# Ranking experts in halves of 64 tokens, with the first tile's rows turned before the next tile's query

## The reference, cut to what matters

```
q = (hc @ w_query).reshape(128, 8, 2, 64)                 # 8 heads, two half keys
s = einsum('chpd,hpnd->chpn', q, sub_keys)                # 128 scores for each half key
s_top, i_top = top_k(s, 16)
cand = s_top[:, :, 0, :, None] + s_top[:, :, 1, None, :]  # 16 x 16 pairs per head
cand_id = i_top[:, :, 0, :, None] * 128 + i_top[:, :, 1, None, :]
best, pos = top_k(cand, 16)
eid = take_along_axis(cand_id, pos); gate = softmax(best)
u = take(u_tab, eid)                                      # 8 x 16 rows of 1024 for each token
act = gelu(einsum('chkd,cd->chk', u, hc)) * gate
out = einsum('chk,chkd->cd', act, take(v_tab, eid))
```

## Time and profile before

| | |
|---|---|
| median of 3 runs | 3320.21 us |
| profiled execution: span, first to last instruction | 3317.3 us |
| the same against the median | 2.9 us below |
| PE busy | 2336.2 us (70%) |
| DVE busy | 1679.4 us (51%) |
| POOL busy | 1480.8 us (45%) |
| moved by DMA | 1047.22 MB, 316 GB/s on average |

### The profile page before, as it was taken

The page is one execution under the profiler, slowest core; times in us unless marked ns, Lnnn a source line. Parts: engine busy times, 40 slices in busy tenths (PEclk is TensorE's granted clock), DMA queues, the critical chain, the costliest instruction groups (busy, mean ns, idle before and its releaser), DMA issues.

```text
span 3317.3 us, 36982 instructions
## 1 busy us (share of the span) xinstructions
PE 2336.2 (70%) x12540; PEld 1281.0 (39%) x12540; DVE 1679.4 (51%) x4368; ACT 558.5 (17%) x1179; POOL 1480.8 (45%) x1577
## 2 busy tenths in 40 slices
PE   7899867898999888995465444447898545444444
PEld 5477624365777545764121000004587400000000
DVE  2521576644233586436965444443712795444444
ACT  2320231401100235102240000002511210000000
POOL 1100044444444444430666777771000167777775
PEclk9999978799999898997575555557899755555555
DMA  8967679899999896991999999993233299999998
GB/s 307 352 209 267 238 269 350 304 354 378 362 365 366 323 347 235 363 334 64 375 349 388 409 409 409 409 409 111 70 114 134 84 379 409 409 409 406 409 409 341
DMA packets 325915, 1047.22 MB, mean 316 GB/s; under 512 B 27424, under 2 KB 38752, under 8 KB 325728
## 3 DMA queue, kind: packets, MB, share of 16 engines
q0 software_dynamic: 240192, 880.90, 69.2%
q1 hardware_dynamic: 85536, 163.95, 14.1%
HBM read 1043.70 MB, written 1.05 MB: 315 GB/s over the span
## 4 chain that ended last, share of the span: by engine, by line
PE 49%; DVE 18%; issue 13%; DMA 10%; ACT 3%; PEld 3%; POOL 2%; PEldq 0%; DVEq 0%; ACTq 0%; POOLq 0%
PE ps L404 24%; PE ps L440 12%; DVE UV L1044 8%; DMA UV<-in_v_tab,idxT 7%; PE ps L426 4%; PEld ps L404 3%; ACT arena L1679 2%; PE ps L396 2%; DMA W<-in_w_mod 2%; POOL UV L2157 1%; PE ps L529 1%; PE ps L571 1%; DVE arena L1415 1%; DVE arena L1424 1%; DVE arena L1418 1%
## 5 line engine op out<-in xcount | busy, mean ns | idle before, releaser
L1044 DVE SCALAR_TENSOR_TENSOR UV<-ps,UV 128x1024 f32<-128x1024 f32 x768 | 909.8, 1222 | 833.4 <-PE ps L426 816.3
L2157 POOL DMA_INDIRECT UV<-in_u_tab,idxT x768 | 723.5, 942 | 1182.4 <-DVEq L1510 498.1
L440 PE MATMUL ps<-UV,acts 128*32 128x512 f32 x3072 | 632.5, 908 | 560.3 <-DVE acts L1053 456.6
L2167 POOL DMA_INDIRECT UV<-in_v_tab,idxT x768 | 724.9, 944 | 281.6 <-issue 198.8
L404 PE MATMUL ps<-H,W 128*128 128x256 f32 (+2 forms) x3296 | 668.7, 363 | 36.4 <-ACT H L1679 26.5
L404 PEld LDWEIGHTS ps<-H,W 128*128 128x128 f32 (+1 forms) x3296 | 574.7, 194 | 147.3 <-issue 76.6
L404 PE MATMUL ps<-arena,W 128*128 128x256 f32 (+1 forms) x1632 | 371.6, 385 | 20.4 <-issue 8.6
L440 PEld LDWEIGHTS ps<-UV,acts 128*32 128x32 f32 x3072 | 78.3, 129 | 716.1 <-DVE acts L1053 572.7
L404 PEld LDWEIGHTS ps<-arena,W 128*128 128x128 f32 (+1 forms) x1632 | 304.4, 190 | 103.3 <-issue 53.2
L426 PE MATMUL ps<-hs,selb 32*128 32x512 bf16 x1536 | 208.5, 530 | 153.1 <-DVE UV L1044 153.0
L1679 ACT ACTIVATE gel<-dots 128x2 f32<-128x2 f32 x384 | 77.4, 202 | 1255.9 <-DVE UV L1044 1247.3
(11 more groups left out here) (198 smaller groups left out, 1698.9 us busy)
## 6 DMA issues: line engine op xcount, KB each, us to landing
W<-in_w_in SPq DMA_DIRECT2D x30, 2048.0 KB, 10.1
UV<-in_w_mod POOLq DMA_DIRECT2D x18, 2048.0 KB, 12.3
W<-in_w_ff SPq DMA_DIRECT2D x16, 2048.0 KB, 14.2
UV<-in_w_ada POOLq DMA_DIRECT2D x9, 2048.0 KB, 11.7
W<-in_w_out SPq DMA_DIRECT2D x8, 2048.0 KB, 11.4
W<-in_w_mod POOLq DMA_DIRECT2D x6, 2048.0 KB, 19.9
W<-in_w_query SPq DMA_DIRECT2D x6, 2048.0 KB, 9.2
UV<-in_u_tab,idxT POOLq DMA_INDIRECT x768, 8.8
```

The source lines that it names most:

```text
L440: last = mm(ps[q:q + GROUP, YB, :], acts[:, tok % SLOTS, GROUP - 1 - r:2 * GROUP - 1 - r], Vs[:, tok % SLOTS, hf * 512:(hf + 1) * 512], st ...
L1044: dve.scalar_tensor_tensor(out=Us[:, j, :], in0=ps[:, b:b + 2, :].rearrange("p a b -> p (a b)"), scalar=1.0, in1=Us[:, j, :], op0=MUL, op1 ...
L2157: pool.indirect_dma_start(Us[:, j, :], None, A["u_tab"], off).then_inc(sem(f"u_arrived{j}"), 16)
L2167: pool.indirect_dma_start(Vs[:, j, :], None, A["v_tab"], off).then_inc(sem(f"v_arrived{j}"), 16)
```

## The change

The ranking of a tile is done in two halves r = 0, 1 of 64 tokens. The scores are laid out so that the 128 partitions hold 64 tokens twice, once for each half of the heads; each half has then 8 lists of scores and 4 of pair sums in each partition instead of 16 and 8. A half has 8 steps (two "top", two "pairs", four "keys"), its own turn of expert numbers and gates, and gatherers wait for half a tile. `route_first` ranks only half 0 of tile n before the stream opens; `route_second` begins with half 1 of tile n, beside the stream, and then both halves of tile n + 1. The transposes of tile n's rows now come ahead of the query of tile n + 1, and VectorE and ScalarE make the parts after "top 1" of half 0. The pieces beside the ranking in c0 are placed anew.

```diff
-STEPS = ["residue", "parts", "top 0", ..., "top 3", "pairs 0", ..., "pairs 3", "keys 0", ..., "keys 3", "experts"]
+STEPS = ["top 0", "top 1", "pairs 0", "pairs 1", "keys 0", "keys 1", "keys 2", "keys 3"]
+HALF = P // 2
-                   "n2": [13], "queried": [14, 15], "pairs 0": [16], "pairs 2": [17]}
-        ADDED_AT = {**MODS_AT, "queried": [], "pairs 0": [], "top 1": [14], "top 3": [15], "pairs 2": [16], "keys 1": [17]}
+                   "n2": [13], "queried": [14, 15], "pairs 0": [16], "pairs 1": [17]}
+        ADDED_AT = {**MODS_AT, "queried": [], "top 0": [14], "top 1": [15], "pairs 0": [], "pairs 1": [16], "keys 3": [17]}
 # TensorE
-                while owed[0] >= PACE and seen[0] < min(segment[1], PAIRS * ready[0]):
+                while owed[0] >= PACE and seen[0] < min(segment[1], PAIRS // 2 * ready[0]):
...
-                        last = mm(o[p][:, hh * P:(hh + 1) * P], qp[64 * p:64 * p + 64, h, in_h(n)],
-                                  keys[64 * p:64 * p + 64, h, :], start=True, stop=True)
+                for i in range(4):
+                    for b in range(2):
+                        h, at = 4 * a + 2 * b + i % 2, n % 2 * P + i // 2 * HALF
+                        for p in range(2):
+                            last = mm(o[p][HALF * b:HALF * b + HALF, i * P:(i + 1) * P], qp[64 * p:64 * p + 64, h, at:at + HALF],
+                                      keys[64 * p:64 * p + 64, h, :], start=True, stop=True)
...
-                    beat((STEPS[i], n), (4.4 if i < 6 else 3.2) if n == 1 else 12.4 if i < 6 else 7.6)
+                    beat((step, n, r), {"top": 4.4, "pairs": 3.2, "keys": 2.0}[what] if n < 2 else {"top": 12.4, "pairs": 7.6, "keys": 4.6}[what])
...
-                pe.transpose(o[:, 0:P], eid, ident[:, :])
-                full(pe.transpose(o[:, P:2 * P], gat.rearrange("p a b -> p (a b)"), ident[:, :]), ("ij", n))
+                for b in range(2):
+                    q = slice(HALF * b, HALF * b + HALF)
+                    mm(o[q, 0:HALF], eid[q, f], ident[q, q], start=True, stop=True)
+                    last = mm(o[q, HALF:P], gat.rearrange("p a b -> p (a b)")[q, f], ident[q, q], start=True, stop=True)
...  # route_first
                     scores(n, u)
+                hidden(n, hold)
                 mods_at(tag, "queried")
                 for u in range(2):
                     query(tag, n + 1, u)
-                hidden(n, hold)
-                routes(n)
+                routes(n, 0)
...  # route_second
+                rows_by_pair(n - 1, [0])
+                routes(n - 1, 1, {"top 0": [lambda: rows_by_pair(n - 1, range(1, 8))]})
                 for a in range(2):
-                    rows_by_pair(n - 1, [a])
                     scores(n, a)
                 if tag == "x0":
                     stream("tile 1 done", max(seen[0], 2 * PAIRS + 2))
-                routes(n, {"top 0": [lambda: rows_by_pair(n - 1, range(2, 8))], **beside})
+                for r in range(2):
+                    routes(n, r, beside.get(r, {}))
...
-            BESIDE = {"top 1": [lambda: hidden(1, bank)], "top 2": [lambda: norm("f", "n1"), lambda: rows_after(1)],
-                      "top 3": [lambda: first_products(0)], "pairs 2": [lambda: first_products(1)]}
+            BESIDE = {0: {"top 1": [lambda: hidden(1, bank)], "pairs 1": [lambda: norm("f", "n1"), lambda: rows_after(1)],
+                          "keys 1": [lambda: first_products(0)]}, 1: {"top 0": [lambda: first_products(1)]}}
 # VectorE: every step works on slice hh of 4 heads instead of all 8, for example
-                    sixteen_best(top, tix, sc, [(i, i) for i in range(4 * e, 4 * e + 4)])
+                    sixteen_best(top, tix, sc, [(i, i) for i in range(8 * r + 4 * e, 8 * r + 4 * e + 4)])
...
-                routes(n, 2)
-                hidden(n)
+                routes(n, 0, {"top 1": [lambda: hidden(n)]})   # hidden: residue, wait part2, third part, wait parts_ready
...
+                routes(n - 1, 1)
                 for a in range(2):
                     beat("sc", n, a)
...
+                for r in range(2):
+                    routes(n, r, beside.get(r, {}))
 # ScalarE, route_first
+                hidden(n)
+                beat("ht", n)
                 mods_at(tag, "queried")
                 for u in range(2):
                     query(n + 1, u)
-                hidden(n)
-                beat("ht", n)
-                routes(n)
-                second_part(n)
+                routes(n, 0, {"top 1": [lambda: second_part(n)]})
 # ScalarE, routes: spreads ranks and takes exponentials of one half at a time; route_second as on TensorE
 # GpSimd
-                if 2 * g % P == 0:
-                    pool.wait_ge(sem("idx_ready"), 2 * g // P + 1)
+                if 2 * g % HALF == 0:
+                    pool.wait_ge(sem("idx_ready"), 2 * g // HALF + 1)
```

More of the change, by code:

```diff
@@ L829, in routes @@
-            def routes(n, beside={}):
-                for i in range(2, len(STEPS) - 1):
-                    beat((STEPS[i], n), (4.4 if i < 6 else 3.2) if n == 1 else 12.4 if i < 6 else 7.6)
-                    if n == 0:
-                        mods_at("c0", STEPS[i])
-                    for piece in beside.get(STEPS[i], ()):
+                for i in range(4):
[4 more added lines that the diff above has]
+                                      keys[64 * p:64 * p + 64, h, :], start=True, stop=True)
+                            if (i, b) == (3, 1):
+                                full(last, ("sc", n, a, p))
@@ L836, in routes @@
+                beat(("sc", n, a), 2.0)
+            def routes(n, r, beside={}):
+                for step in STEPS:
+                    what = step.split()[0]
+                    beat((step, n, r), {"top": 4.4, "pairs": 3.2, "keys": 2.0}[what] if n < 2 else {"top": 12.4, "pairs": 7.6, "keys": 4.6}[what])
+                    if (n, r) == (0, 0):
+                        mods_at("c0", step)
+                    for piece in beside.get(step, ()):
                         piece()
                 pe.wait_ge(sem("routed"), nxt("routed"))
-                o = bank(("ij", n))
@@ L844, in route_first @@
+                full(last, ("ij", n, r))
+                ready[0] = 2 * n + r + 1
+                ready_at[2 * n + r] = seen[0]
             def route_first(tag):
@@ new lines, in sum_ranks, with hidden @@
+                    o = eqp[:, hh, 0:r, :] if r > 1 else ij[:, a, hh, :].unsqueeze(2)
+                    link(dve.tensor_tensor(out=o, in0=eqp[:, hh, 0:r, :], in1=eqp[:, hh, r:2 * r, :], op=ADD))
+            def hidden(n):
+                for a in range(2):
+                    dve.wait_ge(sem("part1"), 2 * n + a + 1)
+                    p = full_bank(dve, ("ht", n, a))
+                    link(dve.tensor_tensor(out=hres[:, a * 512:(a + 1) * 512], in0=p, in1=hp1[:, a * 512:(a + 1) * 512], op=SUB))
+                    dve.sem_inc(free(("ht", n, a)), 1)
+                dve.sem_inc(sem("residue"), 1)
+                dve.wait_ge(sem("part2"), n + 1)
+                dve.tensor_tensor(out=hp3, in0=hres, in1=hp2, op=SUB).then_inc(sem("parts_ready"), 1)
+                dve.wait_ge(sem("parts_ready"), n + 1)
@@ new lines, in route @@
+            def route(n, r, step):
+                what, e = step.split()[0], int(step.split()[-1])
+                hh, f = slice(4 * r, 4 * r + 4), slice(HALF * r, HALF * r + HALF)
+                if what == "top":
+                    dve.wait_ge(sem("scores_ready"), 4 * n + 2 * e + 2)
+                    sixteen_best(top, tix, sc, [(i, i) for i in range(8 * r + 4 * e, 8 * r + 4 * e + 4)])
+                    if e == 1:
+                        dve.tensor_copy(tixb[:, 8 * r:8 * r + 8, :], tix[:, 8 * r:8 * r + 8, :]).then_inc(sem("ranked"), 1)
@@ L1512, in hidden @@
-            def hidden(n):
-                route(n, "residue")
-                route(n, "parts")
-            def routes(n, at, beside={}):
-                for step in STEPS[at:-1]:
-                    route(n, step)
-                    beat(step, n)
-                    if n == 0:
+                        link(dve.scalar_tensor_tensor(out=eid[:, f], in0=ij[:, 0, hh, :].rearrange("p a b -> p (a b)"), scalar=float(NKEY),
+                                                      in1=ij[:, 1, hh, :].rearrange("p a b -> p (a b)"), op0=MUL, op1=ADD))
@@ L1523, in routes @@
+            def routes(n, r, beside={}):
+                for step in STEPS:
+                    route(n, r, step)
+                    beat(step, n, r)
+                    if (n, r) == (0, 0):
                         mods_at("c0", step)
@@ L1525, in routes @@
                         piece()
-                route(n, "experts")
+                experts(n, r)
             def route_first(tag):
```

161 lines of the change are left out of this document (68 added, 93 removed).

## The result

| | before | after |
|---|---|---|
| time, median (range) | 3320.34 us (3319.95 to 3325.86, 4 runs) | 3363.39 us (3362.43 to 3369.49, 4 runs) |
| ratio to before | | 1.0125, 95% interval 1.0111 to 1.0139 |
| span of the profiled execution | 3317.3 us | 3360.7 us |
| VectorE busy, instructions | 1679.4 us, 4368 | 1706.8 us, 4566 |

The change costs 43 us, 1.25%. The forecast was slower by 27.6, to 3347.8 us, with a range of 3322 to 3370. The medians in this document are over all runs and the ratios over the fast ones: of e12's five runs one took 5813 us, and of the eight of the kernel before beside it one took 3687.

What follows compares the result with a forecast made beforehand. The bound was taken to change by stage: gathers in the long streams, TensorE's dense products between, TensorE and VectorE by turns in c0. c0 +35.6, x0 -4, x1 -4 make +27.6 on 3320.2: 3347.8 us, range 3322 to 3370.

Steps and rivals of the forecast that it cites:

- The price of a half: Ranking one half takes 28.0 us, two take 56, 7 more than a whole tile; bounds 24.5 and 31.5 a half.
- Scores: 16 products of 64x64x128 replace 8 of 64x128x128: 0.6 us extra taken for each half of the heads, bounds 0 and +1.16.
- c0: First stretch: tile 1 starts 27.4 us later, its ranking adds 13.7, fewer later visits return 5.5: +35.6 us in all.
- 7, 2.5 and 4: Tile 1 in c0: 7 us for its halves, 2.5 for one more visit, 4 for the first product's lost cover.
- The wait for the second part: At x0 and x1 VectorE newly waits 8 to 9 us for ScalarE's second part; experts come only 3.7 us earlier.
- The opening at x1: Stream start before tile 4: -3.7 earlier experts, -5 gather start, +4.7 beside the stream, -4 us, between -13 and +4.
- The opening at x0: Stream start before tile 2: the same sum as at x1 holds, -4 us.
- opening -5, beside the stream +4.7: At x0 and x1: earlier gather start gains 5 us (0 to 9.4); three halves beside the stream, 26 visits, lose 4.7 more.
- 1 (VectorE sets c0's pace, 3325): In c0 TensorE's pieces slip wholly into VectorE's time, +13 in place of 35.6: 3325 us; chance 0.13.
- 2 (the transfers swallow the delay): Gathers and weights bound 430 to 1500, so only the stream's start counts, -1.5 there: 3311 us, faster; chance 0.10.
- 3 (VectorE bounds both openings, +6 each): At x0 and x1 halves take 31.5 us with no pairs in reserve, +6 each instead of -4: 3368 us; chance 0.15.
- 4 (no earlier start): At x0 and x1 the second part comes 4 us later still: 3355 us; chance counted within the forecast's 0.62.

Runs made afterwards that it cites:

- e12: e10 with 7/5 of the time counted for each ranking step in TensorE's order, so more visits lie between steps: 3512.87 us, 0.9944 of the kernel before.
- e5: The changed kernel with tiles 0 and 1 ranked in one piece again, tile 0's parts behind its ranking: 3585.77 us, 1.0083 of the kernel before.
- e3: e2 with both halves of tile 0 ranked before the stream opens, the last four modulation products spread over them: 3322.47 us, 0.9997 of the kernel before.
- e1: The changed kernel with residues, second and third part moved back behind the ranking of the first half: 3350.95 us, 1.0075 of the kernel before.
- e2: The changed kernel with parts early: residues between the score sets, second part before the next query's copies, third behind "top 0": 3342.61 us, 1.0052 of the kernel before.
- e11: e10 with 6/5 of the time counted for each ranking step in TensorE's order, so more visits lie between steps: 3536.25 us, 0.9968 of the kernel before.
- e10: e2 with tiles 0, 1, 3 and 5 ranked in one piece, only 2 and 4 in halves; e7 repeated: 3551.9 us, 1.0006 of the kernel before.
- e4: e3 with tiles 2 and 4 also ranked in both halves before their streams open: 3367.65 us, 1.012 of the kernel before.
- e7: e2 with tiles 0, 1, 3 and 5 ranked in one piece, only 2 and 4 in halves: 3554.33 us, 0.9992 of the kernel before.
- e8: The kernel before, without the change, profiled again on a chip with gathers at 353 GB/s: 3560.32 us.

## Why the prediction was right, and where its sizes were off

The forecast was 27.6 and the landmarks give 43.4. The difference of 15.8 is made up of 3.8 ahead of the change, 3.6 in c0, 8.2 at x0 and 0.2 in the rest.

**The price of a half: right.** 28.0 and three visits of 2.5 make 35.5 us; from experts to experts tile 0's second half took 35.1 (430.53 to 465.63). The slope of the earlier trace rows holds: an operation on 128x64 took 0.22 us, on 128x128 0.29. VectorE's busy time rose by 27.4 us in all, where six tiles by 7 would be 42; the 7 holds 0.84 us of waiting for each tile's second turn, and gaps between instructions (there are 198 more of them), which the busy time doesn't count.

**Scores: the value taken was wrong, to no effect.** The 16 products of 64x64 (32 instructions in the trace) took 1.10 us at full clock, the 8 of twice the columns of weights (16 instructions) 1.16. The extra is 0, not 0.6. The Trainium skill's rule of four independent 64x64 tiles (TensorEngine Tiling (Array Packing), Available Configurations) holds here. At 468.19 they took 1.98, at a granted clock of 0.5 (1.2 GHz); at 1558.36 it was 1.0 (2.4 GHz).

**c0: mechanism right, size 3.6 us short.** Forecast +35.6, measured +39.2 behind the common 3.8. Taking 3.8 off each landmark: experts at 426.8 (forecast 428.4), tile 1's first step at 469.4 (467.5), first product of the first block at 596.1 (about 591). The first miss is a visit that got in ahead of "top 0" and scores at half the clock: it was granted at 0.50 from 444 to 477, where TensorE was busy for 13.61 of 33 us. The second is tile 1, 128.5 us from its first step where the terms make 125.8 (they are 7, 2.5 and 4, whose sum is 13.5 and not the 13.7 that I wrote). What TensorE makes up behind it was taken as 5.5 and is 6.6; a visit in the earlier trace rows takes 1.32 us and not 1.37. e5 shows the whole to be the halves of tiles 0 and 1: with them gone c0 is 1.1 us from before. e3 splits it: 18 us return when only the early opening goes, not the 28 to 30 that I expected. Of that gap 7.8 us are the wait for ScalarE's spread, which a half is too short to hide; the rest is open.

**The wait for the second part: right, at x0 1.4 to 2.4 us too short.** 10.39 us at x0 and 9.08 at x1, in place of 8 to 9; experts 3.9 us sooner after the first search at x0 (44.7 for 48.5, forecast -3.7), 5.2 at x1. e1 and e2 confirm it: with the parts early it is 33 us.

**The opening at x1: right in sum, in part by luck.** -4.4 with -4 forecast. The terms are the time by which the experts come earlier, -5.2 for -3.7; the full rate lost in the first 19 to 23 us of the stream, 9.4 us before and 4.1 now, -5.3 for -5; and the rate lost beside the ranking behind it, 6.5 before (376 of 409 GB/s for 80 us) and 13.1 now (370 for 137), +6.6 for +4.7. The first and the last miss nearly cancel.

**The opening at x0: wrong, +4.2 for -4.** The step that failed is "opening -5, beside the stream +4.7". By GB/s below 409, the kernel before lost 13.0 us from 1566 to 1672 (359); now 1606 to 1767 at 354 loses 21.7. So both terms together are +8.7 where I had -0.3. I had carried x1's rows over to x0. The opening had less to give there: 6.9 us were lost in its first 24 us before (292 GB/s), and 4.8 now, -2 for -5. And beside the ranking 82 us at 379 GB/s, 6.0 us lost, became 142 at 360, 17.0 lost: +11 for +4.7. At x1 the two together are 17.2 against 15.9, +1.3. Behind the opening the gathers run at 360 GB/s beside x0's halves and at 370 beside x1's. VectorE is busy for 91 to 92% of the time in both, so it is near its bound there, but what makes x0 slower by 10 GB/s no run separates; it stays open. e11 and e12 bear on it at 353 GB/s: with more visits between the same steps x0, from its second norm to x1's first, took 865.8 and 857.3 us, where e10 took 877.5.

**The rivals.** 1 (VectorE sets c0's pace, 3325): fell, VectorE busy 98 of 129 us. 2 (the transfers swallow the delay): fell, 602 to 1160 is unchanged. 3 (VectorE bounds both openings, +6 each): its price nearly came at x0 (+4.2) and not at x1 (-4.4), though VectorE was busy for 128.63 of 142 and 125.83 of 137 us behind the two openings. At 353 GB/s the openings cost 12 and 15 us, but VectorE was busy for only 141 of 205 us, so that isn't the rival's mechanism. 4 (no earlier start): fell, by 3.9 and 5.2 us of earlier experts.

## What to carry to other kernels

Cutting a ranking into halves pays only where something waits for the first half, and only once the steps of other engines on its path have been moved out of it as well: here the early opening was worth 20 and 25 us at two places against two halves in a row (e4 against e3), and 10 and 15 us against a whole ranking (e2 against the kernel before, at 409 GB/s). A 10 us wait for one cast on ScalarE, the overhead of the halves and a 39 us loss at a third place, where nothing could use it, took more. Cut at the places that gain, keep the others whole: at 353 GB/s this came out even (e7), at 409 it was not run. When a consumer of gathered data shares an in-order queue with long other work, count how many consumptions lie between the long steps, and look at whom the queue of gathers waits for: this was worth 15.6 us by changing numbers alone (e11), and perhaps 8 more (e12), both at 353 GB/s.

## What the runs showed of the hardware that I had not expected

What gathers reach differed with the chip: 409 GB/s in a stream on those of the first runs, about 353 on those of e5 to e12. The dense stretch of the first block was alike (TensorE busy 521.5 of 559 us in e8, 523.7 of 558 before, at 355 and 356 GB/s), but c0 as a whole took 1172.9 us in e8 and 1147.2 before, so it was slower too. Each chip was seen at one time only, and what else ran beside the kernel's core isn't on record; so a busy neighbour is a rival to the chip itself, and nothing here decides between them. The verdict on a change that lies beside gathers can differ with it either way: the same halves at x1 gave -4.4 us at 409 GB/s, and +15.2 and +10.4 at 353.

The other surprise was in the order of things on ScalarE. A step of VectorE that got shorter did not end sooner in e3, since what it was handed by ScalarE (the spread of ranks, 7.76 us late) stood behind a copy that waited for TensorE. The same wait came out in e1 at x0, with 3.67 us. The longer step had hidden this without anyone having placed it so.
